# A hybrid mLSTM + SSD + mixture-of-experts step on one core: the mixer's work put in another order

## What is computed

```
hn = rmsnorm(h) ; u = hn @ w_in                      # xa, za, i, f, zb, x/B/C, dt
q, k, v per head from silu(conv(xa)) and xa          # 8 mLSTM heads of 128
h_a = mLSTM(q, k, v, i, f)                           # scores * exp(dmat - m), state C, n, m
h_a = h_a * rsqrt(mean(h_a^2) + eps) * norm_a * sigmoid(za)
xs, B, C = silu(conv(x/B/C)) ; dt = softplus(dtr)    # 16 SSD heads of 64, state 128, 2 groups
y = SSD(xs, dt, A, B, C) + d_skip * xs
y = group_rmsnorm(y * silu(zb)) * norm_b
h = h + concat(h_a, y) @ w_out
h = h + moe(rmsnorm(h))                              # 4 groups x 4 experts, top-1 group, top-2 experts
y_out = rmsnorm(h)                                   # and all new states are outputs
```

## Time and profile before

| | us |
|---|---|
| median of 3 runs | 933.55 (930.46 to 938.48) |
| the profiled execution, its whole time | 930.9 |
| its span, first to last instruction | 929.2 |
| TensorE busy | 830.6 |
| VectorE / ScalarE / GpSimd busy | 316.4 / 149.8 / 104.2 |
| mean granted TensorE clock | 0.955 |

### The profile page before, as it was taken

How to read it: one execution, slowest core, us unless ns; L and a number is a source line. 1 busy time by engine, 2 the same in 40 slices (tenths; PEclk the granted TensorE clock), 3 DMA queues, 4 the chain that set the end, 5 groups by cost and what they waited for, 6 DMA issues and landing times.

```text
span 929.2 us, 9631 instructions
## 1 busy us (share of the span) xinstructions
PE 830.6 (89%) x3774; PEld 443.0 (48%) x3774; DVE 316.4 (34%) x635; ACT 149.8 (16%) x368; POOL 104.2 (11%) x135
## 2 busy tenths in 40 slices
PE   5999999998587789999999899989899788999785
PEld 4888788665344458875332243322433223333221
DVE  3966601699978740043002012002111020020203
ACT  2222211543211220051110010100000100101002
POOL 5000000574644410000000000000000000000000
PEclk9999999998677779989999999999999999999999
DMA  8834333568565424930799999999999999999992
GB/s 241 269 113 159 134 115 136 159 194 247 155 183 161 130 84 183 358 115 1 303 409 410 409 409 410 409 409 409 409 409 409 409 409 410 409 409 410 409 409 105
DMA packets 110067, 263.01 MB, mean 283 GB/s; under 512 B 7127, under 2 KB 46219, under 8 KB 110009
## 3 DMA queue, kind: packets, MB, share of 16 engines
q1 hardware_dynamic: 107856, 257.94, 74.2%
q0 software_dynamic: 1648, 3.33, 1.2%
q10 hardware_dynamic: 520, 1.15, 0.4%
HBM read 251.66 MB, written 10.91 MB: 283 GB/s over the span
## 4 chain that ended last, share of the span: by engine, by line
PE 60%; DMA 14%; DVE 13%; SPq 8%; issue 2%; ACT 2%; ACTq 0%; DVEq 0%
PE bank L1421 13%; PE bank L1736 13%; DMA ring<-in_w_up 10%; PE bank L1788 8%; SPq L557 8%; PE bank L1638 6%; PE bank L1718 6%; DVE shared L1090 4%; PE bank L1751 3%; DMA ring<-in_w_down 2%; PE bank L1603 2%; DVE ring L1114 2%; DVE h_tok L1109 2%; PE bank L1560 1%; DVE YS L1118 1%
## 5 line engine op out<-in xcount | busy, mean ns | idle before, releaser
L1736 PE MATMUL bank<-ring,arena 128*64 128x512 f32 x1024 | 226.8, 594 | 26.4 <-DMA ring<-in_w_up 20.1
L1736 PEld LDWEIGHTS bank<-ring,arena 128*64 128x64 f32 x1024 | 73.3, 137 | 176.9 <-issue 131.6
L1421 PE MATMUL bank<-arena,ring 128*128 128x280 f32 x576 | 136.2, 399 | 0.8 <-ACT arena L797 0.8
L1788 PE MATMUL bank<-ring,arena 128*64 128x512 f32 x512 | 113.6, 595 | 14.6 <-ACT arena L942 14.2
L1421 PEld LDWEIGHTS bank<-arena,ring 128*128 128x128 f32 x576 | 109.4, 190 | 27.6 <-issue 1.2
L1355 DVE TENSOR_TENSOR arena<-bank,arena 128x512 f32<-128x512 f32 x16 | 11.1, 692 | 244.2 <-PE bank L1736 244.2
L1788 PEld LDWEIGHTS bank<-ring,arena 128*64 128x64 f32 x512 | 36.4, 137 | 81.6 <-issue 78.9
L1638 PE MATMUL bank<-arena,ring 128*128 128x264 f32 x256 | 59.6, 394 | 0.0
L434 DVE COPY arena<-bank 64x512 f32<-64x512 f32 x16 | 10.9, 683 | 137.9 <-PE bank L1788 137.9
L1718 PE MATMUL bank<-arena,xn 128*128 128x256 f32 (+1 forms) x192 | 54.2, 412 | 0.7 <-DVE arena L1327 0.7
L1638 PEld LDWEIGHTS bank<-arena,ring 128*128 128x128 f32 x256 | 49.5, 195 | 9.3 <-issue 0.7
(11 more groups left out here) (336 smaller groups left out, 749.2 us busy)
## 6 DMA issues: line engine op xcount, KB each, us to landing
ring<-in_w_gate SPq DMA_DIRECT2D x32, 2048.0 KB, 21.1
ring<-in_w_up SPq DMA_DIRECT2D x32, 2048.0 KB, 23.5
ring<-in_w_down SPq DMA_DIRECT2D x32, 2048.0 KB, 19.8
ring<-in_w_in SPq DMA_DIRECT2D x9, 2048.0 KB, 8.7
ring<-in_w_out SPq DMA_DIRECT2D x4, 2048.0 KB, 8.0
out<-h_tok SPq DMA_DIRECT2D x16, 512.0 KB, 3.5
h_tok<-in_state_ssm SPq DMA_DIRECT2D x8, 512.0 KB, 5.2
h_tok<-in_state_mlstm_C SPq DMA_DIRECT2D x8, 512.0 KB, 5.2
```

The costliest lines, as they stand in the source:

```text
L1421: last = mm(bank[n % 4][:, 0:T], slot_k(u % MR, 512)[:, k, o:o + P], hT[:, k, :], start=(k == 0), stop=(k == KD - 1))
L1736: last = mm(b[CAP * half:CAP * (half + 1), :], XG[:, k, e * CAP:(e + 1) * CAP], w[:, kk, half * 512:(half + 1) * 512], start=(k == 0), sto ...
L1788: last = mm(bank[5][CAP * half:CAP * (half + 1), :], HT[:, kk, u * CAP:(u + 1) * CAP], w[:, kk, half * 512:(half + 1) * 512], start=(u == ...
```

## The change

The arithmetic of the layer stays, but the mixer's order and the engines that do its parts are changed. Line numbers are of the kernel before.

- **Tiles.** Only 12 of the 36 tiles are made ahead of the heads: 8 of xa and 4 of x. The other 8 x/B/C tiles are made one in each mLSTM head, the 16 gate tiles (zb, then za) one in each SSD head (the first just ahead of them), all through bank 5 alone; each waits until the bank's last use is read (`b5_free`). Unit order: xa, xa, q/k/v weights, three x/B/C, two zb, two za, four w_out. There are two conv tiles in each mLSTM head.
- **Convolution.** The first tap goes to ScalarE (Identity with scale and bias), three stay on VectorE; conv weights are halved once, and x·sigmoid(x) becomes (tanh(x/2)+1)·x/2. The gates likewise use tanh(z/2); norm scales use Sqrt and a reciprocal instead of ln and exp.
- **States.** C states go by head (8 samples of one head in a buffer), in the mLSTM heads; SSM states by sample, in the SSD heads. The decay goes from GpSimd to ScalarE, as 8 copies with a scale for each state; VectorE adds rows times a column in 8 instructions for each state. C·q is 8 matmuls of one weight column each, into spare columns of banks 0 and 1, copied out and turned by small matmuls (`c_sum`). The v rows go to DRAM and back head by head.
- **GpSimd** computes nothing in the heads but the 8 one-column copies; it still issues small stores.
- **GT** is read from PSUM and not copied; x weighted for the state is made by ScalarE; squares are summed in the heads; the mLSTM scales and part of the products are done in the last SSD heads.
- **Output projection.** It starts right after the last SSD head with units 0 and 1 on six of eight banks, and the remaining norms lie between its parts; the last w_out unit is loaded behind three expert units.

The core of the diff:

```diff
-WIN = [O_XA, O_XA + 512, O_XBC, O_XBC + 512, O_XBC + 1024, O_ZA, O_ZA + 512, O_ZB, O_ZB + 512]
+WIN = [O_XA, O_XA + 512, None, O_XBC, O_XBC + 512, O_XBC + 1024, O_ZB, O_ZB + 512, O_ZA, O_ZA + 512]
+UNIT_SLOT = [0, 1, 2, 0, 1, 0, 1, 2, 0, 1, 2, 0, 1, 2]
+N_EARLY = 12
# SyncE
+            v_rows(0)
+            for h in range(HA):
+                row_load(h + 4)
+                if h + 1 < HA:
+                    v_rows(h + 1)
+                state_step(h)
+                if h == 1:
+                    mixer_unit(U_B + 2)
+                if h == 3:
+                    mixer_unit(U_Z)
+                if h == 6:
+                    mixer_unit(U_Z + 1)
+            mixer_unit(U_Z + 2)
...
+            expert_unit(0, 0, s.y_ps, HB)
+            expert_unit(0, 1, s.yb_norm, KD)
+            expert_unit(0, 2, s.yb_norm, KD)
+            mixer_unit(U_OUT + 3)
# ScalarE, an mLSTM head
+            for h in range(HA):
+                first_tap(3 + 2 * h)
+                first_tap(4 + 2 * h)
+                tanh_of_conv(2 + 2 * h)
+                if h + 1 < HA:
+                    head_in(h + 1)
+                decay_exp(h + 1)
+                tanh_of_conv(3 + 2 * h)
+                decay_state(h + 1)
+                evac(HA + XBC_A[h])
...
+                cq_copy(h)
+                head_out(h)
...
+            act.wait_ge(s.xdt_ready, 3)
+            act.wait_ge(s.out_conv, 16 * 6)
+            for h in range(HB):
+                if h + 1 < HB:
+                    decay_exp(HA + h + 1)
+                if h % 2 == 0:
+                    weighted_x(h // 2)
+                elif h + 1 < HB:
+                    decay_state(HA + h // 2 + 1)
+                z_tanh(h)
# VectorE
+            for h in range(HA):
+                dve.wait_ge(s.sc_ps, h + 1)
+                weighted(h, bank[4])
...
+                c_update(h)
+                conv_taps(3 + 2 * h)
+                if h + 1 < HA:
+                    sample_q_k(h + 1)
+                conv_gate(2 + 2 * h)
+                conv_taps(4 + 2 * h)
+                conv_gate(3 + 2 * h)
...
+                if h % 2 == 0 and h >= 2:
+                    ssd_out(dve, c - 1)
+                    gate_y(c - 1)
+                    s_read(c - 1)
+                if h % 2 == 1:
+                    s_update(c)
+                if h < KD:
+                    dve.wait_ge(s.z_sig, h + 1)
+                    v.scalar_tensor_tensor(out=ZB[:, h, :], in0=ZB[:, h, :], scalar=1.0, in1=bank[5][:, 0:T],
+                                           op0=ALU.add, op1=ALU.mult).then_inc(s.b5_free, 1)
+                if h % 2 == 1 and h >= 9:
+                    num_out((h - 9) // 2)
# TensorE, an mLSTM head
+                if h + 1 < HA:
+                    head_proj(h + 1)
+                if h >= 1:
+                    squares_sum(h - 1)
+                xbc_tile(XBC_A[h])
+                c_read(h)
# TensorE, output
+            out_unit(0)
+            out_parts(range(4), (5, 4))
+            head_rows(4)
...
+            out_parts(range(4), (1, 2))
+            out_unit(1)
...
+            pe.wait_ge(s.yb_norm, KD)
+            out_parts(range(4), (3, 7)).then_inc(s.wo_unit, 1)
```

More of the change, by code:

```diff
@@ L884, in _ @@
-            act.wait_ge(s.cq_ps, NB + 1)
-            a.activation(NUM[:, :, NP:T], bank[3][:, 0:64].rearrange("p (b h) -> p h b", h=HA), ACT.Copy)
-            a.activation(QN[:], bank[3][:, 0:64], ACT.Square).then_inc(s.cq_sb, 1)
-            act.wait_ge(s.sq_ps, HA + KD)
-            a.activation(YSC, bank[7][32:32 + NG, 0:T], ACT.Ln, bias=epst[32:32 + NG, 0:1], scale=1.0 / (D // NG))
-            for half in range(2):
+                if c >= 3:
+                    act.wait_ge(s.sq_ps, HA + 1 + c - 2)
@@ L988, in _ @@
                             .then_inc(s.ht_ready, 1)
+            dve.wait_ge(s.ht_ready, 2)
+            for j in range(2):
+                v.memset(bank[j][:, QT:QT + P], 0.0).then_inc(s.ht_ready, 1)
             dve.wait_ge(s.prev_ps, 2)
@@ L1412, in _ @@
             last.then_inc(s.u_ps, 3)
-            for n0_, (kind, c, u, o) in enumerate(UT):
+            for n0_ in range(N_EARLY):
                 n = n0_ + 3
+                _kind, _c, u, o = UT[n0_]
                 if o == 0:
@@ new lines, in _ @@
+            last.then_inc(s.sq_ps, 1)
+            out_parts((2, 3), (6, 0))
+            pe.wait_ge(s.sst_ready, 2)
+            head_rows(6)
+            out_parts(range(4), (1, 2))
+            out_unit(1)
+            head_rows(7)
+            out_parts((4, 5), (5, 4, 6, 0, 1, 2))
+            pe.wait_ge(s.ysc_ready, 1)
+            pe.wait_ge(s.num_ready, HA)
+            for j in range(NG):
+                mm(bank[7 if j == 0 else 3][:, 0:T], ident[64:64 + NG, 64 + j:65 + j].to_broadcast([NG, P]), YSC,
+                   start=True, stop=True).then_inc(s.gbc_ps, 1)
@@ L1677, in _ @@
+            for dt in range(5, 8):
+                out_turn(dt)
             for i, (t0, m) in enumerate(TOK):
```

901 lines of the change are left out of this document (484 added, 417 removed).

## The result

The changed kernel takes 893.89 us (median of 4 runs, 892.26 to 895.32), beside 934.75 us (930.46 to 938.48, 4 runs) for the kernel before on the same chip: ratio 0.956, 95% interval 0.952 to 0.961. The forecast of 902 us is 8 us too slow; the range of 882 to 924 holds the time. The edits further down ran on other chips, each beside the kernel before, whose medians there were 934.0 (a1 to a4), 932.8 (b1 to c2) and 931.1 (d1, d2). So compare kernels of different chips by their ratios to before.

What follows compares the result with a forecast made beforehand. With tiles laid beside the heads TensorE was mostly the bound: output projection ends at 369, not 403.7 us, 34.7 earlier, less 3 for the clock, 31.7. From 930.9 that gives 899.2, as a median 902; range 882 to 924.

Steps and rivals of the forecast that it cites:

- The limits: Mixer before: tiles fill TensorE alone, mLSTM heads fill TensorE and VectorE, the stage from 250 to 330 us fills neither.
- C·q at 1.75 us: mLSTM heads: 16 C·q passes at 0.11 us each, 1.75 us within TensorE's 14.1 us a head.
- The first head: After twelve tiles, head 0 runs from 67.4 to 91.3 us, TensorE idling some 5 of these 24.
- rival A: mLSTM heads: a serial chain through SP's queue and the v rows makes each 18 us; gain 5, 929 us; chance 0.13.
- The eight-copy decay: ScalarE's decay of one state as eight copies: 2.0 us taken, from 1.2 to 2.9, still covered at 2.9.
- The wait on `out_conv`: Joint before the SSD heads: ScalarE waits for GpSimd's stores, delaying gate tile 1 by 4 us (0 to 6).
- SSD heads at 5.7 us: A pair of SSD heads takes 11.4 us, with TensorE at 5.4 and VectorE at 5.1 a head; fifteen take 85.5.
- The contention price: VectorE's arguments in SSD heads: 597 ns without GpSimd's work beside them, not 1248; the contended row makes it 15 us longer.
- B: VectorE and ScalarE set the SSD head, by single bank and contended prices: 7.0 us, gain 12, 922; chance 0.15.
- C: Slower: TensorE waits for bank 5 every SSD head and stays at 1.2 GHz: 78 us more, 980; chance 0.05.
- D: Tanh and exp alternate by 1.28 us table loads, four a head: about 10 us more, 912; inside the forecast and B.
- The two ends of the gain, 45 and 61 us: Whole kernel: no loss at joints and a shorter middle gain 45 us, 888; no TensorE idle at all, 61, 872.

Runs made afterwards that it cites:

- a1: Changed kernel with ScalarE's wait on `out_conv` moved behind the tanh of the first gate tile: 885.0 us, ratio to before 0.949.
- a4: Changed kernel with Sigmoid in place of Tanh in the convolution and the gates: 905.29 us, ratio to before 0.968.
- b1: Changed kernel with C·q of all eight samples written to row 0 of its bank, not rows 0, 32, 64, 96: 899.19 us, ratio 0.964.
- c2: a1 with denominators and head scales behind VectorE's read of bank 5, and all decays given back to GpSimd: 889.87 us, ratio 0.954.
- d1: a1 with denominators and head scales behind VectorE's bank 5 read, and gate tanh ahead of weights and decay in every SSD head: 887.63 us, ratio 0.952.
- d2: d1 with the denominators in three portions (behind heads 1, 3 and 4) and head scales behind head 6: 882.24 us, ratio 0.946.
- a3: Changed kernel with all parts of the output projection put back behind the norms: 909.69 us, ratio to before 0.975.
- a2: Changed kernel with all 16 state decays given back to GpSimd, one whole-tile product each: 888.58 us, ratio to before 0.954.

## Why the prediction was right, and where its terms were off

Each length is counted from the first tile, so the start falls out. The chain of waits of the kernel after gives the pieces:

```profile
24.19 45.28 PE bank L1516 x192
...
79.61 1.20 DMA v_dram<-VS
80.82 3.46 DMA arena<-v_dram
84.35 2.19 DVE h_tok L1147 x8
88.62 2.25 ACT h_tok L826 x8
...
197.42 3.03 DMA out<-ring
200.99 1.52 ACT ring L896 x6
203.33 7.00 PE bank L1528 x16
```

| step | forecast, us | measured, us |
|---|---|---|
| twelve tiles | 45.3 | 45.3 |
| first head, to the end of its denominator passes | 22.8 | 20.4 |
| mLSTM heads 1 to 7 | 102.1 | 91.4 (7 x 13.06) |
| last denominator passes to first y | 15.7 | 16.6 |
| first y to output projection | 96.3 | 103.7 |
| output projection | 65.0 | 63.9 |
| clock, apart | 3 | in the steps |
| sum | 350.2 | 341.3 |

(The prediction rounded 304.3 to 304 at the last SSD head; the steps here add up without that.) The start then takes back 1.9 us (24.0 for 22.1) and everything behind the last output matmul 2.8, most of it the two lengths of the experts told above, which leaves the profiled execution at 895.3, beside a forecast of 899.2 for it. The closeness is in part luck: the mLSTM heads came 13.1 us shorter than forecast, and the SSD heads with their joint 8.3 longer.

**The limits: right.** The argument was that TensorE's tiles and the heads' other engines each had a stage of their own, and that laid side by side TensorE is the bound. TensorE is busy for 265 of the 277 us from first tile to output projection. GpSimd has 26.6 us in the whole kernel. The 13.5 us of norms alone are gone, and a3 prices that part at 13.4 us of mixer (14.9 in its own stages).

**C·q at 1.75 us: wrong, and the largest miss.** I priced it by a chain of passes that all write one place. They take 0.55 on the chain, 1.2 us less in each of eight heads; b1, with all of them on one row, gives the 1.84 us that the price stood for. Seven heads of it are 8.4 of the 10.7 us, and a period of 14.1 less 1.2 is the 12.85 that was measured. The other 2 us are in the last heads, where I had added 3.4 for transposes.

**The first head: total nearly right, its reason wrong.** I had TensorE wait some 5 us for `c_update(0)` behind the v rows (3.45 + 3.36 us). The trip took 1.20 + 3.46. C·q began at 86.97, straight behind the interleaved tile, and TensorE idled 1.0 us only, for ScalarE's copy of C·q, which stood behind the eight-copy decay (88.62, 2.25 us, 2.43 in the timeline). From head 1 on TensorE waits for nothing until the joint, so rival A did not come, as its counter-argument of 11 us of lead said.

**The eight-copy decay: 2.0 us taken, 2.43 measured** (385 ns each, 0.30 in a row; bounds 1.2 to 2.9, the lower of which no row showed). ScalarE was busy 57.6 of 89 us in the heads, 8.3 a head for the 8.4 forecast. Only the start of the queue made it late once, and a2 and a4 show that this is where ScalarE's work costs something.

**The wait on `out_conv`: right in place and size (4 us; 4.46), short by the clock.** The slow tile behind it is 3.0 us more. I had kept 3 us for the clock in all, for the first head and this pause. It took some 8: 3.0 here, 1.7 in the second slow tile (233.21), 1.7 at the joint (2.43 and 4.73 us, for 1.50 and 3.94 in b1), and 1.6 behind the 1.0 us of idle time in the first head (3.59 us for the 1.99 of a2). a1 shows the pause and both slow tiles of the SSD heads together: 8.1 us.

**SSD heads at 5.7 us: too low by 0.3.** From 241.4 to 301.5 ten of them take 60.1 us with TensorE never idle. A pair of heads on TensorE in the kernel after:

```profile
265.00 4.04 PE L1528 MATMUL bank<-arena,ring 128*128 128x280 f32 x16
268.97 0.73 PE L1734 MATMUL bank<-ring,ident 8*128 8x280 f32 x2
269.63 1.13 PE L1767 MATMUL bank<-shared,ring 128*64 128x272 f32 x6
270.69 4.04 PE L1528 MATMUL bank<-arena,ring 128*128 128x280 f32 x16
274.57 1.02 PE L1753 MATMUL bank<-xn,ring 128*128 128x128 f32 x6
275.52 0.62 PE L1724 MATMUL bank<-ring,strip 128*2 128x272 f32 x2
276.07 1.13 PE L1767 MATMUL bank<-shared,ring 128*64 128x272 f32 x6
277.13 0.74 PE L1528 MATMUL bank<-arena,ring 128*128 128x280 f32 x2
```

From 265.00 to 277.13 it is 12.13 us. I had TensorE at 5.4 a head: the tile takes 3.9 to 4.0 among other work, not 3.77; the broadcast of a head's scales (0.66 in every second head, 268.97 to 269.63) was missing; state block and sum take 1.5 a pair, not 1.3. What I had as the limit, VectorE's read of the single bank, is none once the burst is over. The denominators and scales, priced at 5.8 us, cost pauses of 1.41 and 2.08 us, and the second of them 1.7 more in the slow tile behind it. So the stage's 7.4 us over the forecast are 4.7 of two slow tiles, 4.5 of the heads, 0.5 at the pause, less 2.3 of the denominators.

**The contention price: right, and it did not decide.** I took 597 ns over 1248 for the widest block and said that the contended price would be 15 us longer. It measures 480 to 490, and 1433 beside GpSimd (a2). The exclusive lock on the shared ports that the prediction cited from the Trainium skill (SBUF — State Buffer, "Who interferes with whom") agrees with both. At that price the mLSTM heads stayed as they were, since TensorE's 12.85 us of a head cover it. In the SSD heads of a2 the block took 702 ns on average and the stage grew by 2.7 us, so the full contended price there, with a head of 6.0 us, was not tried.

**Rivals B, C and D.** B's place, the single bank, is where all pauses of the SSD heads are, but it cost 2.08 us at most behind the first pause, not 1.3 in every head. The clock was 1.00 from 241 on and 0.88 in the first five SSD heads (0.95 over the stage). The latter is under the 0.9 that the prediction named as a sign of being wrong; it came from two slow tiles, so C did not come. (C's own sum is short: six heads at the half clock are 31.2 us, not yet the 31.7 of the gain; it takes seven.) D was ruled out by the absence of loads. a4's 11 us are near the 10 that the prediction gave D, but by luck: it counted four loads a head and a full ScalarE, and the heads kept their length. The two ends of the gain, 45 and 61 us, are not worked out in the prediction, so nothing here can be held against them.

## What to carry to other kernels

When two stages have different full engines, merge them and then add up only the engine that is full in the sum. A saving on another engine (the contended VectorE blocks, 15 us by their rows) belonged to some 20 us in the old order; in the new one the decays on either engine come out the same. With work spaced evenly over heads, look next for bursts and for the starts of queues: six small operations of 4.2 us in one place held the gate bank up, moving them whole moved the hole and made it larger, and splitting them closed it. A wait belongs at the first instruction that really needs it, not at the head of a queue. Price a pause of TensorE with the half-clock work that may stand behind it (4.5 us idle, 3.0 more for the next tile; 2.1 us idle, 1.7 more in one kernel and nothing in another). And read an edit's worth from the stage that it touches, since the stages ahead of it differ by up to 3 us between profiles of the same program.

## What was not expected of the hardware

- Sixteen one-row passes whose outputs lie 32 rows apart take 0.55 us, and 1.84 us when all write row 0.
- The same 16 gate passes in front of the first tile took 3.93 us in some profiles and up to 6.7 in others, at a granted clock that the records give as 1.00 in both. What causes it stays open. The first tile's start lies anywhere within 4.5 us, so single profiles are to be compared from a later mark.
- The tile behind a pause of TensorE took 7.00 us behind 4.46 (granted clock 0.57), 5.73 behind 3.45 and behind 2.88 (0.69), 5.73 behind 2.08 in one kernel (0.70) and 4.04 behind 2.09 in another (1.00).
- ScalarE's first tap of the convolution, an Identity with scale and bias from memory, took 645 ns for 304 columns; a tanh of the same width took 456.
- The product of the samples' read-out, of one shape throughout, took 1088 ns in the earlier trace rows, 686 with GpSimd idle, and 792 in a2, where GpSimd decays beside it.
